# Eighteen pieces of small TensorE work in the two mixers of a hybrid decoder step, moved to neighbouring places

## The chip, the cores and the metric

One core of a Trainium2 chip runs the whole program in one launch. The metric is the device time of that launch in microseconds (us). All tensors are float32.

## The reference, cut to what matters

A trunk of two layers is run once on a prompt of 256 tokens and once on 8 samples of one token each (264 columns together). A layer is: SwiGLU half step, mixer, SwiGLU half step, each behind an adaLN norm whose shift, scale and gate come from a conditioning vector.

```
for l in range(DEPTH):
    mod = (c @ w_ada[l] + b_ada[l]).reshape(B, N_SUB, 3, D_MODEL)
    h = ada_norm(x, norm_gain[l, 0], mod[:, 0, 0], mod[:, 0, 1])
    x = x + 0.5 * mod[:, 0, 2] * swiglu(h, w_ffn_in[l, 0], w_ffn_out[l, 0])
    h = ada_norm(x, norm_gain[l, 1], mod[:, 1, 0], mod[:, 1, 1])
    y, sa, scv, sh, sc = mixer_block(h, ...)
    x = x + mod[:, 1, 2] * y
    h = ada_norm(x, norm_gain[l, 2], mod[:, 2, 0], mod[:, 2, 1])
    x = x + 0.5 * mod[:, 2, 2] * swiglu(h, w_ffn_in[l, 1], w_ffn_out[l, 1])
```

The mixer has three branches: A (HGRN2: gated linear recurrence, 4 heads of 128), B (causal convolution and RG-LRU) and C (GLA: gated linear recurrence, 4 heads of 64 keys). Each recurrence gives outputs for the prompt and a final state (`S_t = diag(f_t) S_{t-1} + k_t v_t^T`, `o_t = S_t^T q_t`), and one step from a given state for each sample. The branch outputs are gated, merged and multiplied with `w_out`.

## The kernel before, in words

**Weights and products.** Every weight tile is loaded in float32 by a DMA of SyncE (SP), 512 KB mostly, into one of 6 slots of `raw` (`load`, L430). ScalarE (ACT) rounds it to a high part `whi` (`split_hi`, L449), VectorE (DVE) subtracts to a low part `wlo` (`split_lo`, L457), and TensorE (PE) does three products for each 128x128 block (`mm3`, L492 to L494). Such a tile is a *unit*, usually 24 matmuls of 264 columns. There are 218 units in a layer, 82 of them in the mixer. ACT and DVE prepare unit u+3 at the start of their step u, when PE has ended unit u-1; 4 slots of `whi` and `wlo`. The load of place c in SP's queue waits until the tile of place c-6 has been read by DVE (a unit) or by PE (an adaLN tile).

**The mixer's units**, in order: 0 to 3 `f`, 4 to 7 `bx`, 8 to 11 `i` (values of A), 12 to 15 `q`, 16, 17 `cq`, 18, 19 `ck`, 20 `bg`, 21 `rg wa`, 22 to 24 `bg`, 25 `rg wx`, 26 to 29 `cv` (values of C), 30 to 33 `cg`, 34 to 37 `ag`, 38 to 45 `ma`, 46 to 57 `mb` pairs with a branch unit `b` behind each (48, 51, 54, 57), 58 to 61 `mc`, 62 to 65 branch `a`, 66 to 69 `mc`, 70 to 73 branch `c`, 74 to 81 `w_out`. A unit writes one of three PSUM banks (a branch unit writes two); PE waits until the group three back in the same rotation has been read.

**Small work on PE** stands behind the matmuls of a unit, at a place that a table gives. In PE's loop over units (`mixer`) it is issued in this order: ca, alpha, transposes of the values of A and C (`values_T`, L854), levels of A then of C, a samples' output (`sample_o`, L910), then for A and after it for C: outputs (L869, L870), head sums (L918), spread (L931), transposed keys (L879), final state (`final_state`, L888); last the tail's transposes (L1042) and the adaLN group (`ada_units`, L678).

- `MIX_ADA` (L52): the four places of the adaLN groups. A group is 4 tiles, each with 4 products into 32 columns of the array (32 matmul records), and computes half of one block of 1024 outputs: the shift and the scale of the norm behind the mixer. Its four loads stand in SP's queue right behind the load of the unit three places on (`load_order`). After the second and the fourth group DVE turns the block into `mod` (`to_mod`, L1725), and after the fourth makes the gains too, at its step place+2 (`ada_ends`), last of that step.
- `AT` (L122): places of the rest, DVE's and ACT's part at the step after. `C_vT` (32, 34): the 2x4 transposes of C's values; ACT copies them at 33 and 35. `A_S` 63: the final state of A, ACT copies it at 64. `so` (24, 28, 38, 44, 47, 52): the samples' outputs of six batches of states; a batch waits for `st_new`, DVE's add of the decayed state and the outer products, which is made at its steps 24, 27, 36, 41, 46, 51.
- `PE_LV` (L239): the nine levels of each recurrence's score matrix. Level i+1 on PE waits for DVE's `keep` and `update` of level i, done at the step after level i's place. The last C level (54) is needed by C's outputs at 56.

**The samples' outer products.** DVE turns A's sample values at step 16; POOL (GpSimd) writes them to DRAM (`rows_out`, L1145), and when they have landed reads them back broadcast over the partitions (`outer`, L1159); ACT scales them by the keys at step 21 for batch 0 and at step 26 for batch 1; DVE adds them to the state at step 24 and 27; PE's output of batch 0 stands behind unit 24, of batch 1 behind unit 28. ACT and DVE take their work in order, so a wait of ACT at step 21 holds its later splits.

**The end of the mixer.** For each branch `c` unit DVE gates two tiles straight from PSUM and adds them to `tmp` (L2103, L1646, four operations). ACT makes the high part, POOL (tiles 0 to 5) or DVE (6, 7) the low part. Unit 74 takes two banks at once, those of the tiles 5 and 6 of branch `c`. In DVE's step u the split of unit u+3 stands first, the gating of unit u behind it, `ada_ends` last.

```
for u, (kind, what, j) in enumerate(MIX):
    n_unit = unit(L, "mix", u)
    if (what, j) != ("o", 0):
        split_lo(dve, n_unit + LOOK)
    ...
    ada_ends(L, "mix", u - 2)
```

Of the kernel before, what the change touches and what calls it, by code (L numbers as in the profile page):

```python
# [48 lines left out]
    return l * UNITS + BASE[stage] + k  # L49


MIX_ADA = (10, 16, 29, 71)  # L52
ADA_BLOCKS = [(0, 1), (0, 0)]
ADA_FIRST = {}
RING = 8
# [3 lines left out]
def plan_ada():  # L59

    for l in range(NL):
        for f, places, blocks in (
                (0, (("in0", 16), ("in0", 28), ("in0", 41), ("out0", 11)), [(l, 2), (l, 3), (l, 4), (l, 5)]),
                (1, (("in1", 18), ("in1", 36), ("out1", 11)), [(l, 8), (l + 1, 0), (l + 1, 1)])):
            if f:
                for n, place in enumerate(MIX_ADA):
                    ADA_FIRST[(l, "mix", place)] = (8 * len(ADA_BLOCKS) + 4 * n, 4)
# [51 lines left out]
LOAD_AT = {load: c for c, load in enumerate(LOADS)}  # L119


AT = {'ca': 9, 'alpha': 11, 'A_vT': 14, 'A_sT': 16, 'C_sT': 30, 'C_vT': (32, 34), 'A_out': 50, 'C_out': 56, 'A_kT': 59, 'A_S': 63, 'C_kT': 68, 'C_S': 70, 'tailT': 73, 'kv': (23, 26, 35, 40, 45, 50), 'st_f': ((13, 14), (15, 16), (31, 32), (36, 37), (43, 44), (48, 48)), 'k_v': ((21, 21), (26, 26), (34, 35), (39, 40), (44, 45), (49, 50)), 'so': (24, 28, 38, 44, 47, 52), 'st': (14, 17, 33, 37, 44, 48)}  # L122
EARLY_AT = {'A_abs': 7, 'A_ln': 9, 'A_ls': 9, 'A_exp': 10, 'A_k': 11, 'A_f': 10, 'C_z': 10, 'C_ln': 15, 'C_ls': 16, 'C_f': 19, 'conv': (9, 10, 14, 15), 'conv_hi': 18, 'conv_lo': 19, 'A_qs': 15, 'C_qs': 17}
HEAD_AT = {'A': {'sq': 51, 'ms': 52, 'root': 54, 'inverse': 54, 'spread': (55, 56), 'scaled': (56, 58), 'high': 59, 'low': 59}, 'C': {'sq': 57, 'ms': 59, 'root': 62, 'inverse': 62, 'spread': (64, 67), 'scaled': (64, 67), 'high': 67, 'low': 67}}

# [36 lines left out]
def mixer_groups():  # L162

    out = []
    for u, (kind, what, j) in enumerate(MIX):
# [5 lines left out]
        elif kind == "br":  # L171
            out += [(e, "br" + what, 2 * j + n, u) for n in range(2)]
        out += [("V", "so", i, u) for i in (4, 5) if AT["so"][i] == u]
    return out
# [61 lines left out]
LEVELS = [0, 1, 2, 4, 8, 16, 32, 64, 128]  # L236


PE_LV = {'A': (17, 20, 24, 28, 31, 33, 38, 43, 45), 'C': (24, 28, 33, 38, 43, 45, 47, 50, 54)}  # L239
RG_AT = {'tanh': 22, 'gate': 25, 'exp': 26, 'square': 28, 'scaled': 30, 'root': 29, 'u': 32, 'scan': 32, 'y': 35, 'high': 37, 'low': 37}  # L240


# [3 lines left out]
def trunk(nc, x_prompt, x_sample, c_prompt, c_sample, state_hgrn, state_conv, state_rglru, state_gla,  # L246
# [4 lines left out]
    with ctx:  # L251
# [150 lines left out]
        def wait(eng, name, L, i=0):  # L402

            eng.wait_ge(S[name], L * PER[name] + i + 1)
# [62 lines left out]
        def group_done(eng, L, stage, g):  # L467

            g += G_BASE[(L, stage)]
            e = EV[g]  # L470
            eng.wait_ge(evac[e], ev_count(e, g + 1))
# [164 lines left out]
        def _(pe):  # L636
# [148 lines left out]
            def ca_sums(L):  # L785

                pe.wait_ge(alpha_in, (L + 1) * 80)
                for j in range(4):
                    for kt in (2 * j, 2 * j + 1):
                        last = mm(AUX[3][32 * j:32 * j + 32, 0:NT], wca[:, kt, :], tmp[:, kt], start=(kt % 2 == 0),  # L790
                                  stop=(kt % 2 == 1))
                last.then_inc(S["ca_mm"], 1)

            def alpha(L):

                wait(pe, "ca_done", L)
                pe.wait_ge(set_pool, 4)
                for jj in range(2):
                    last = mm(AUX[2][:, jj * 256:jj * 256 + 256], wal[:, jj * P:(jj + 1) * P],
                              ca[:, 0:256], start=True, stop=True)  # L800
                for jj in range(2):
                    last = mm(AUX[3][:, jj * 8:jj * 8 + 8], wal[:, jj * P:(jj + 1) * P],
                              ca[:, 256:264], start=True, stop=True)
                last.then_inc(S["C_alpha"], 1)
# [87 lines left out]
            def sample_o(L, i, bank):  # L892
                br, j = BATCHES[i]
                wait(pe, "st_new", L, i)
                if i == 0:
                    wait(pe, "A_sc", L, 0)
                    wait(pe, "A_qs", L)
                else:
                    wait(pe, "soe", L, i - 1)
                if i == 2:  # L900
                    wait(pe, "C_vTe", L, 1)
                if i == 5:
                    wait(pe, "A_oe", L)
                if i == 4:
                    wait(pe, "C_qs", L)
                for e in range(1 if br == "A" else 2):
                    rows_ = slice(0, P) if br == "A" else slice(64 * e, 64 * e + 64)
                    q_ = qs[rows_, j if br == "A" else 4 + j]
                    for n in range(4):
                        last = mm((AUX[1], bank)[e][32 * n:32 * n + 32, 0:256].rearrange("p (b v) -> p b v", b=NB), q_,  # L910
                                  st[rows_, i % 2, :, 32 * n:32 * n + 32], start=True, stop=True)
                last.then_inc(S["so"], 1)
# [22 lines left out]
            def mixer(L):  # L935
                g = [0]

                def take_bank():
                    if g[0] < 3:
                        group_done(pe, L, "out0", 4 + g[0])  # L940
                    if g[0] >= 3:
                        group_done(pe, L, "mix", g[0] - 3)
                    g[0] += 1
                    return BK[(g[0] - 1) % 3]


                for u, (kind, what, j) in enumerate(MIX):
# [46 lines left out]
                    if u == 2:  # L994
# [6 lines left out]
                        group_done(pe, L, "out0", KT - 1)  # L1001
                    if u == AT["ca"]:
                        ca_sums(L)
                    if u == AT["alpha"]:
                        alpha(L)
                    if u == AT["A_vT"]:
                        wait(pe, "rows_evac", L)
# [3 lines left out]
                    for t in range(2):  # L1011
                        if u == AT["C_vT"][t]:
                            if t == 0:
# [5 lines left out]
                    for br in "AC":  # L1019
                        for li in range(9):  # L1020
                            if u == PE_LV[br][li]:
                                level(L, br, li)
                    for i in range(6):
                        if u == AT["so"][i]:
                            sample_o(L, i, take_bank() if i >= 4 else None)
# [618 lines left out]
        def _(dve):  # L1644
# [265 lines left out]
            def mixer(L):  # L1910
# [107 lines left out]
                for u, (kind, what, j) in enumerate(MIX):  # L2018
# [150 lines left out]
                    for br in "AC":  # L2169
                        for li in range(9):  # L2170
                            if u == PE_LV[br][li] + 1:
                                keep(br, li)
# [145 lines left out]
```

## Time and profile before

| what | value |
|---|---|
| median of 3 runs (lowest, highest) | 1465.27 us (1463.87, 1466.27) |
| the profiled execution, its time and span | 1464.36 us, span 1462.6 us |
| PE busy, weight loads, DVE, ACT, POOL | 98%, 94%, 63%, 55%, 6% of the span |
| mean granted clock of PE | 0.994 |
| share of PE in the chain that ended last | 89% |
| DMA | 323.77 MB, mean 221 GB/s |
| mixer of layer 0, of layer 1 (first unit to last) | about 253 to 536 us, 964 to 1250 us |

PE's busy share says little alone: matmuls overlap, each record is about 0.28 us long and a new one starts every 0.12 us. What an interruption costs is read from the distance between starts. A row of the timeline merges equal instructions that follow one another; in brackets stands the idle time of the engine before it and what ended it.

### The profile page before, as it was taken

Reading aid. Unit: us, or ns where it says so; the run is one execution under the profiler, and the core shown is the slowest. Engines: PE = TensorE matmul, PEld = TensorE weight load, DVE = VectorE, ACT = ScalarE, POOL = GpSimd, SP = SyncE. Lnnn points to the kernel's source line nnn. Section 1 sums busy time; section 2 is a strip of 40 time slices with the busy share of each in tenths; the row PEclk is TensorE's granted clock in tenths of the full one; section 3 lists DMA queues with packets and bytes.
Section 4 is the critical chain, followed back from the end, with each engine's and each line's share of the span. In section 5 each row is a group of like instructions: output and inputs, shape, how many; then the busy total and the mean of one; then the engine's idle time right before and its main releaser. Section 6 shows DMA issues by size and latency. Waiting matters only on the chain.

```text
span 1462.6 us, 33414 instructions
## 1 busy us (share of the span) xinstructions
PE 1433.3 (98%) x14126; PEld 1372.0 (94%) x14126; DVE 923.8 (63%) x1572; ACT 807.5 (55%) x1337; POOL 86.9 (6%) x131
## 2 busy tenths in 40 slices
PE   6999999999999999999999999999899999999998
PEld 4999999998999999999999999999899999999998
DVE  3564546778876677555575554577797677855553
ACT  2554435886666466444464444468766655644543
POOL 1030000001110110000000000000011002000000
PEclk9999999999999999999999999999999999999999
DMA  9988897688884669788668888777889557775661
GB/s 341 292 260 265 249 265 196 174 251 256 228 228 142 191 176 293 217 248 252 185 202 264 271 269 266 189 187 209 234 238 268 164 152 208 219 241 157 180 187 41
DMA packets 460039, 323.77 MB, mean 221 GB/s; under 512 B 11220, under 2 KB 435708, under 8 KB 459891
## 3 DMA queue, kind: packets, MB, share of 16 engines
q1 hardware_dynamic: 452240, 299.96, 70.0%
q0 software_dynamic: 6880, 20.41, 4.9%
q8 instruction: 112, 1.84, 0.5%
q10 hardware_dynamic: 770, 1.27, 0.2%
q14 instruction: 37, 0.30, 0.1%
HBM read 313.29 MB, written 8.37 MB: 220 GB/s over the span
## 4 chain that ended last, share of the span: by engine, by line
PE 89%; ACT 3%; DMA 3%; DVE 2%; issue 2%; SPq 1%; POOL 0%; DVEq 0%; ACTq 0%; POOLq 0%
PE bank L492 27%; PE bank L493 26%; PE bank L494 26%; PE bank L678 4%; DMA xA<-v_rows 1%; SPq L550 1%; ACT xA L1222 1%; ACT whi L449 1%; DMA v_rows<-vrA 1%; DMA raw<-in_w_ffn_in 1%; DVE st L1646 1%; PE bank L869 1%; PE bank L888 1%; DVE wlo L457 0%; PE bank L910 0%
## 5 line engine op out<-in xcount | busy, mean ns | idle before, releaser
L457 DVE TENSOR_TENSOR wlo<-raw,whi 128x1024 fp32r<-128x1024 f32 (+1 forms) x436 | 518.6, 1203 | 357.9 <-ACT whi L449 356.8
L492 PE MATMUL bank<-hH,whi 128*128 128x264 f32 x2048 | 588.6, 287 | 1.1 <-DVE hL L1646 0.6
L493 PE MATMUL bank<-hL,whi 128*128 128x264 f32 x2048 | 582.0, 284 | 0.0
L494 PE MATMUL bank<-hH,wlo 128*128 128x264 f32 x2048 | 581.3, 284 | 0.0
L449 ACT ACTIVATE whi<-raw 128x1024 fp32r<-128x1024 f32 (+1 forms) x436 | 442.1, 1033 | 187.7 <-PE bank L494 178.3
L492 PEld LDWEIGHTS bank<-hH,whi 128*128 128x128 f32 x2048 | 387.1, 189 | 14.9 <-issue 13.6
L493 PEld LDWEIGHTS bank<-hL,whi 128*128 128x128 f32 x2048 | 387.5, 189 | 0.0
L494 PEld LDWEIGHTS bank<-hH,wlo 128*128 128x128 f32 x2048 | 385.6, 188 | 0.0
L492 PE MATMUL bank<-hidH,whi 128*128 128x264 f32 x704 | 201.1, 286 | 0.0
L494 PE MATMUL bank<-hidH,wlo 128*128 128x264 f32 x704 | 200.1, 284 | 0.0
L493 PE MATMUL bank<-hidL,whi 128*128 128x264 f32 x704 | 199.5, 283 | 0.0
L492 PEld LDWEIGHTS bank<-hidH,whi 128*128 128x128 f32 x704 | 132.4, 188 | 1.6 <-issue 1.2
L1222 ACT ACTIVATE hidH<-hid 128x264 fp32r<-128x264 f32 x88 | 37.3, 424 | 173.1 <-DVE hid L1646 173.0
L494 PEld LDWEIGHTS bank<-hidH,wlo 128*128 128x128 f32 x704 | 132.7, 188 | 0.0
L493 PEld LDWEIGHTS bank<-hidL,whi 128*128 128x128 f32 x704 | 132.3, 188 | 0.1
L492 PE MATMUL bank<-uH,whi 128*128 128x274 f32 x320 | 94.4, 295 | 0.0
L493 PE MATMUL bank<-uL,whi 128*128 128x274 f32 x320 | 92.8, 290 | 0.0
L494 PE MATMUL bank<-uH,wlo 128*128 128x274 f32 x320 | 92.4, 289 | 0.0
L1222 ACT ACTIVATE sil<-bank 128x264 f32<-128x264 f32 x76 | 29.8, 392 | 96.4 <-PE bank L494 96.4
L492 PE MATMUL bank<-yH,whi 128*128 128x264 f32 x256 | 73.8, 288 | 1.3 <-DVE gA L2103 1.3
L494 PE MATMUL bank<-yH,wlo 128*128 128x264 f32 x256 | 72.7, 284 | 0.0
L493 PE MATMUL bank<-yL,whi 128*128 128x264 f32 x256 | 72.6, 284 | 0.0
(323 smaller groups left out, 1656.8 us busy)
## 6 DMA issues: line engine op xcount, KB each, us to landing
raw<-in_w_ffn_in SPq DMA_DIRECT2D x176, 512.0 KB, 4.8
raw<-in_w_in SPq DMA_DIRECT2D x120, 512.0 KB, 4.8
ring<-in_w_ada SPq DMA_DIRECT2D x96, 512.0 KB, 6.6
raw<-in_w_ffn_out SPq DMA_DIRECT2D x64, 512.0 KB, 4.8
raw<-in_w_ada SPq DMA_DIRECT2D x32, 512.0 KB, 4.3
raw<-in_w_ffn_out SPq DMA_DIRECT2D x32, 384.0 KB, 4.7
first<-in_w_ada SPq DMA_DIRECT2D x16, 512.0 KB, 12.3
raw<-in_w_out SPq DMA_DIRECT2D x16, 512.0 KB, 4.9
```

The costliest lines, as they stand in the source:

```text
L449: nc.scalar.activation(whi[:, s, 0:w], raw[:, r, 0:w], ACT.Copy).then_inc(hi_done, 1)
L457: nc.vector.tensor_tensor(wlo[:, s, 0:w], raw[:, r, 0:w], whi[:, s, 0:w].bitcast(F), ALU.subtract).then_inc(lo_done, 1)
L492: nc.tensor.matmul(out, a, rh, start=start, stop=False)
L493: nc.tensor.matmul(out, a, rl, start=False, stop=False)
L494: return nc.tensor.matmul(out, b, rh, start=False, stop=stop)
L550: sp.dma_start(first[:, n], src).then_inc(first_in[FIRST_OF[n]], 16)
L678: last = mm(ps[32 * j:32 * j + 32, 0:256].rearrange("p (b i) -> p b i", i=32), cst[:, kt], src[:, j], start=(kt == 0), stop=(kt == KT - 1))
L869: mm(o, v0, sc[br][:, h, 0:T], start=True, stop=False)
L888: last = mm(AUX[base][0:dk, h * P:(h + 1) * P], KTT[br][:, t, h * dk:(h + 1) * dk], VT[br][:, t, h * P:(h + 1) * P], start=(t == 0), stop= ...
L1222: return nc.scalar.activation(out, in_, func, **k)
L1646: tt = lambda o, i0, i1, op: v.tensor_tensor(o, i0, i1, op)
```

## The change

Nine entries of three tables get a new value, for both mixers. Nothing is added or taken away; the arithmetic is the same.

```diff
-MIX_ADA = (10, 16, 29, 71)
+MIX_ADA = (11, 17, 28, 70)
...
-AT = {... 'C_vT': (32, 34), ... 'A_S': 63, ... 'so': (24, 28, 38, 44, 47, 52), ...}
+AT = {... 'C_vT': (31, 33), ... 'A_S': 64, ... 'so': (24, 28, 38, 43, 47, 52), ...}
...
-PE_LV = {'A': (17, 20, 24, 28, 31, 33, 38, 43, 45), 'C': (24, 28, 33, 38, 43, 45, 47, 50, 54)}
+PE_LV = {'A': (17, 20, 24, 28, 31, 33, 38, 43, 45), 'C': (24, 28, 33, 38, 43, 45, 47, 50, 52)}
```

Where each piece stands then: adaLN groups behind alpha (11), behind A's level 0 (17), behind two levels and the samples' output of batch 1 (28), behind C's final state (70). C's value transposes in front of A's level at 31 and of two levels at 33. A's final state in front of C's first spread (64). The samples' output of batch 3 behind two levels (43). C's last level in front of the samples' output of batch 5 and A's head sums (52). The steps of ACT and DVE that follow a place, and the adaLN loads in SP's queue, move with it.

## Rows read from the trace of the kernel before

**Rows 1.** PE's waits: who waited for whom: total us, times, longest

```profile
PE bank L910 <- DVE st L1646: 7.7, 4, 2.5
...
PE bank L492 <- DVE gA L2103: 1.3, 2, 0.7
```

**Rows 2.** PE's timeline: the samples' output of batch 0, layers 0 and 1 (start, us)

```profile
330.46 0.64 PE L910 MATMUL bank<-st,qs 128*32 128x256 f32 x8 [0.72 <-DVE st L1646]
...
1042.93 1.08 PE L910 MATMUL bank<-st,qs 128*32 128x256 f32 x8 [2.09 <-DVE st L1646]
```

**Rows 3.** A window behind the wait at unit 28: us, busy times, PEclk (granted clock), DMA

```profile
346.20:349.60 3.40, 3.40 (x16) 3.40 (x17) 3.37 (x5) 0.00 (x0) 0.00 (x0) 0.50 0.79 255
```

**Rows 4.** PE's timeline: the adaLN group behind unit 16, layer 0 (start, us)

```profile
301.93 0.28 PE L493 MATMUL bank<-hL,whi 128*128 128x264 f32 x1
302.05 0.28 PE L494 MATMUL bank<-hH,wlo 128*128 128x264 f32 x1
302.26 1.93 PE L678 MATMUL bank<-raw,cst 128*32 128x256 f32 x32
304.12 0.39 PE L492 MATMUL bank<-hH,whi 128*128 128x264 f32 x1
304.35 0.29 PE L493 MATMUL bank<-hL,whi 128*128 128x264 f32 x1
```

**Rows 5.** PE's timeline: a samples' output behind a level (38), and alone (44)

```profile
383.45 0.64 PE L910 MATMUL bank<-st,qs 128*32 128x256 f32 x8
384.02 0.39 PE L492 MATMUL bank<-hH,whi 128*128 128x264 f32 x1
...
403.57 0.64 PE L910 MATMUL bank<-st,qs 128*32 128x256 f32 x8
404.14 0.39 PE L492 MATMUL bank<-hH,whi 128*128 128x264 f32 x1
```

**Rows 6.** PE's timeline: eight transposes alone, and eight in front of head sums

```profile
295.50 1.04 PE L854 MATMUL bank<-ident,vA 128*128 128x128 f32 x8
296.29 0.37 PE L492 MATMUL bank<-hH,whi 128*128 128x264 f32 x1
...
460.96 1.04 PE L879 MATMUL bank<-ident,kA 128*128 128x128 f32 x8
461.92 0.65 PE L918 MATMUL bank<-xA,ones 128*32 128x264 f32 x8
```

**Rows 7.** ACT's timeline: step 19 and 21 of layer 0, step 21 of layer 1

```profile
313.11 1.06 ACT L449 ACTIVATE whi<-raw 128x1024 fp32r<-128x1024 f32 x1 [0.61 <-DMA raw<-in_w_in]
...
320.59 2.46 ACT L1222 ACTIVATE xA<-xA,kA 128x128 f32<-128x128 f32 x8 [0.39 <-DMA xA<-v_rows]
...
1033.06 2.46 ACT L1222 ACTIVATE xA<-xA,kA 128x128 f32<-128x128 f32 x8 [1.84 <-DMA xA<-v_rows]
```

**Rows 8.** DVE's timeline, step 17 of layer 0: the low part of unit 20

```profile
308.00 1.23 DVE L457 TENSOR_TENSOR wlo<-raw,whi 128x1024 fp32r<-128x1024 f32 x1 [0.18 <-ACT whi L449]
```

**Rows 9.** SP's loads (L430) issued from 300 to 312 us

```profile
DMA to landing us min/median/max: 3.1/6.1/8.2
```

**Rows 10.** DVE's timeline: steps 71 to 74 of layer 0

```profile
503.82 0.43 DVE L2103 SCALAR_TENSOR_TENSOR gA<-xA,bank 128x264 f32<-128x264 f32 x1 [2.06 <-PE bank L494]
...
508.82 0.43 DVE L2103 SCALAR_TENSOR_TENSOR gA<-XB,bank 128x264 f32<-128x264 f32 x1 [1.60 <-PE bank L494]
...
510.44 1.78 DVE L457 TENSOR_TENSOR wlo<-raw,whi 128x1024 fp32r<-128x1024 f32 x1
512.15 0.41 DVE L2103 SCALAR_TENSOR_TENSOR gA<-XB,bank 128x264 f32<-128x264 f32 x1
...
513.85 0.44 DVE L1725 STREAM_TRANSPOSE adaT<-bank 128x256 f32<-128x256 f32 x1
...
514.74 0.77 DVE L1646 TENSOR_TENSOR yL<-tmp,yH 128x264 fp32r<-128x264 f32 x2
```

**Rows 11.** PE's timeline: the first matmul of unit 74, layer 0

```profile
512.82 0.36 PE L492 MATMUL bank<-yH,whi 128*128 128x264 f32 x1 [0.65 <-DVE gA L2103]
```

More of the change, by code:

```diff
@@ L119 @@
 LOAD_AT = {load: c for c, load in enumerate(LOADS)}
-AT = {'ca': 9, 'alpha': 11, 'A_vT': 14, 'A_sT': 16, 'C_sT': 30, 'C_vT': (32, 34), 'A_out': 50, 'C_out': 56, 'A_kT': 59, 'A_S': 63, 'C_kT': 68, 'C_S': 70, 'tailT': 73, 'kv': (23, 26, 35, 40, 45, 50), 'st_f': ((13, 14), (15, 16), (31, 32), (36, 37), (43, 44), (48, 48)), 'k_v': ((21, 21), (26, 26), (34, 35), (39, 40), (44, 45), (49, 50)), 'so': (24, 28, 38, 44, 47, 52), 'st': (14, 17, 33, 37, 44, 48)}
+AT = {'ca': 9, 'alpha': 11, 'A_vT': 14, 'A_sT': 16, 'C_sT': 30, 'C_vT': (31, 33), 'A_out': 50, 'C_out': 56, 'A_kT': 59, 'A_S': 64, 'C_kT': 68, 'C_S': 70, 'tailT': 73, 'kv': (23, 26, 35, 40, 45, 50), 'st_f': ((13, 14), (15, 16), (31, 32), (36, 37), (43, 44), (48, 48)), 'k_v': ((21, 21), (26, 26), (34, 35), (39, 40), (44, 45), (49, 50)), 'so': (24, 28, 38, 43, 47, 52), 'st': (14, 17, 33, 37, 44, 48)}
 EARLY_AT = {'A_abs': 7, 'A_ln': 9, 'A_ls': 9, 'A_exp': 10, 'A_k': 11, 'A_f': 10, 'C_z': 10, 'C_ln': 15, 'C_ls': 16, 'C_f': 19, 'conv': (9, 10, 14, 15), 'conv_hi': 18, 'conv_lo': 19, 'A_qs': 15, 'C_qs': 17}
```

## The prediction

> **What bounds the kernel now.** I read the chain that ended last first: PE holds most of it, so time is won or lost where PE starts its next matmul later or earlier. PE's waits come next. In the mixers only two kinds are long: the samples' outputs wait four times for DVE's new state, 7.7 us in all, and the first unit of `w_out` waits twice for DVE's gating of branch c, 0.7 us each [rows 1]. Of the four, the one behind unit 24 is 0.72 us in layer 0 and 2.09 in layer 1 [rows 2]; those behind unit 28 take the rest, 2.5 each. The windows show what the first kind costs besides: after the wait at unit 28 the granted clock is 0.50, the 1.2 GHz level, for 3.4 us [rows 3]; half of it, 1.7 us, is lost. The trace has one behind each of the three waits over 2 us; in layer 1 the output of batch 0 itself runs in it (1.08 us instead of 0.64), in layer 0, after 0.72 us, it doesn't [rows 2]. Everything else in the mixer is PE going from unit to unit, and the timeline gives the price of a stop there.
>
> **What a stop costs.** Matmuls of a unit start 0.12 us apart. Before the adaLN group it is 0.21, and after the first matmul behind it 0.23 [rows 4]. So work that uses 32 columns of the array costs itself (304.12 - 302.26 = 1.86 us for the group) plus 0.09 at the entry and 0.11 at the exit. A samples' output takes 0.57 us to the next unit whether it stands alone or behind a level [rows 5], so one that joins saves the 0.20. Full-width work is different: eight transposes take 0.79 us alone plus 0.08 behind them, 0.87 together, and 0.96 when 32-column work follows, 0.09 of it the entry of the follower that is paid anyway [rows 6]. A join with them saves nothing.
>
> The Trainium skill, page TensorE: Matmul & The Clock Gate, section Part 2: What happens when you issue a matmul, speaks against the change: the next weights are pulled ahead and loaded beside a running matmul, so a switch would be hidden. The trace doesn't agree for 32-column work, 0.21 against 0.12 us. By the page all joins would bring 0.0; this is the third rival.
>
> **The change part by part**, for one mixer:
> - adaLN group to 17, to 28, to 70; samples' output to 43; C's last level to 52: each joins other small work: 5 x 0.20 = 1.0 us. The last follows no 32-column work but precedes it; the same pair of edges goes.
> - adaLN group to 11: behind alpha, which is full width: between 0.0 [rows 6] and 0.20 [rows 4]; I take the middle, 0.1.
> - C's transposes to 31 and 33, A's final state to 64: full width in front of narrow work: 0.0 as in rows 6, at most 0.1 each, below nothing only if a wait appears. The four transposes (half of 0.87 us) now delay the level behind them; DVE takes that level a step later, behind a split and a gating, which cover it.
>
> Sum of the joins: 1.1 us. But not all of it reaches the end.
>
> **Absorbed at the samples' outputs.** The 0.3 us of the groups at 11 and 17 lie before the wait at 24. That wait is not set by PE: ACT's products of batch 0 wait for the broadcast that POOL fetched, 0.39 us in layer 0 and 1.84 in layer 1 [rows 7], and DVE's and PE's parts follow ACT's queue from there. PE arrives 0.3 earlier and waits 0.3 longer: nothing is won. The wait at 28 hangs on ACT's queue after unit 26, so it moves with PE and stays 2.5 us [rows 1].
>
> **SP's queue.** Each group takes its four 512 KB loads one place along. At 17 this matters: the load of unit 22 stood behind an adaLN tile six places back and could go at once; now it waits for the low part of unit 20, done at 308.00 + 1.23 = 309.2 us [rows 8]. Loads here land 3.1 to 8.2 us after issue [rows 9], so at 312.3 to 317.4; before, ACT took it at 313.11 [rows 7]. I take 4.5 us (only one 256 KB load stands before it, while the median of 6.1 is of loads queued in a burst): 313.7, so ACT is 0.6 later. In layer 0 ACT has 0.4 of slack before the broadcast, so the samples' output comes 0.2 later; in layer 1 it has 1.8. Against that, POOL's small writes and its broadcast meet two 512 KB loads less in their first 2 us, and may land up to 1 us earlier; only layer 1 can use that. I take +0.2 and -0.2: 0 in all, with 1 us either way for each mixer. At 11 the load of unit 16 goes later in the same way, but DVE's wait for alpha goes 2 us earlier, and ACT has idle time until step 15. At 28 unit 32's load is taken late by ACT and DVE, three units before PE needs it. The groups' own tiles are released a step later, like the group. POOL can fetch the last state batch one unit earlier, since it waits for the output of batch 3; nobody waits for it.
>
> **New at unit 74.** This is the costly part. The group at 71 stood between units 71 and 72, now it stands before unit 71. So unit 71 ends 1.86 us later, while unit 72 ends at the same time as before less 0.20. DVE's gating of unit 71 begins at 503.82 + 1.86 = 505.68 us [rows 10]. Four operations take 510.44 - 508.82 = 1.62, the split behind them 512.15 - 510.44 = 1.71: 509.01, now later than unit 72's end allows (508.82 less 0.20 = 508.62). Four more operations: 510.63. Then comes what stood behind unit 73's gating and moves to step 72: the turn of the adaLN block and the gains, 514.74 - 513.85 = 0.89: 511.52. The next split, 1.71: 513.23, and there the tile's gating starts that stood at 512.15. PE's unit 74 follows 512.82 - 512.15 = 0.67 behind it [rows 10, 11]: 513.90, against 512.82. That is 1.08 us later, and it has already swallowed the 0.20 of the group at 70. The split takes 1.78 us here and 1.23 elsewhere [rows 10, 8]; it is slow while POOL makes low parts beside it. If the second one escaped POOL it would be 0.5 instead of 1.1; if the turn is slowed as well, 1.4. Unit 72 and 73 themselves don't wait: their banks are those of tiles gated two units earlier.
>
> The Trainium skill, page SBUF — State Buffer, section Who interferes with whom, says that a DVE instruction with two SBUF inputs contends with a GpSimd one that reads SBUF. By that rule, the trace agrees (1.78 against 1.23).
>
> **Other queues.** DVE's step 44 has batch 3's output in front of a level's work, whose taker is a unit away; its step 53 gets C's last level from step 55, behind the reading of batch 5, and what follows there is idle time. C's last level at 52 waits for DVE's level 7 of step 51, one unit after the step's start instead of three. No wait of that kind stands in the list of before for a level at such a distance; the nearest bounds are 0 and the 0.7 of the other DVE wait [rows 1]. I take 0, since DVE has a whole unit of PE for four short operations. The turn of the block at step 18 moves to 19, behind the low parts that unit 21 waits for: that helps if anything.
>
> **Sum.** Joins that count: samples' output 0.20, level 0.20, group at 28 0.20: 0.6 us for a mixer. Unit 74: +1.1. Net +0.5, for two mixers +1.0 us. The profiled execution took 1464.36 us (span 1462.6 and 1.8 around it), so this execution would take 1465.3; it stands 0.9 under the median of 1465.27, and the median becomes 1466.2. The measurement can tell about 0.2% (2.9 us) from no change, so I forecast no change.
>
> **Rivals.**
> 1. Joins as priced, and DVE hides the later step 71 (it has 2.06 and 1.60 us of idle time there [rows 10]). For it: idle time exists. Against: it lies before the operands come. Then 2 x (-0.8) = -1.6: 1463.7. Chance 0.17.
> 2. Slower: the late load. If unit 22's load takes the 6.1 us of the median, it lands at 315.3, 2.2 us after 313.11. Layer 0's samples' output is then 1.8 later, layer 1's 0.4 (slack 1.8). Unit 21 waits too, since the low parts of the convolution stand behind unit 22's split in DVE's queue. With +1.0 that is +3.2: 1468.5; at 7 us of landing +5.0. It decides from 5.9 us of landing on. For it: DMA runs near its full rate behind this point. Against: the burst is shorter. Chance 0.13.
> 3. Joins save nothing: +2 x 1.1 = 2.2: 1467.5. Against: rows 4 and 5. Chance 0.05.
> 4. Faster: one slow-clock stretch goes. In layer 1 the wait at 24 is 2.1 us and brings one [rows 2, 3]; in layer 0 it is 0.7 and brings none. If the broadcast lands 1 us earlier the wait is near 1.1: -1.0 - 1.7 + 1.0 = -1.7, and with rival 1's end -4.3: 1461.0. Chance 0.10, half of it over the bound. The stretch could come in layer 0 instead: 1.7 the other way, in the range.
> 5. The change doesn't do what it says: a moved piece waits where it stands now (0.05); no more than 1 us by the slack above.
>
> My own forecast has 0.50. **Chances:** faster 0.10, same 0.78, slower 0.12. **Range:** 1462.5 (joins of full-width work 0.1 each, 0.5 at unit 74, one stretch less) to 1469.5 (rival 2 with 6.5 us).
>
> **What would show it.** PE's timeline: L678 behind L802, L841, L910 and L888 with no unit between; the 0.21 before it gone at 17, 28, 70. PE's wait for DVE's gating is 1.7 to 1.9 us instead of 0.7, and the turn of the block (L1725) in front of the split before tile 6's gating. The waits for the new state about 8.3 us in four, the one at 28 unchanged at 2.5. ACT's idle time before unit 22's split 1.0 to 1.5 us instead of 0.6. The prediction is wrong if unit 74's wait stays at 0.7, if a wait appears at a level, or if the granted clock is low in two or four stretches instead of three.

## The result, and the profile after it

| what | before | after |
|---|---|---|
| median of 20 runs each (lowest, highest) | 1463.93 us (1459.72, 1466.43) | 1467.56 us (1466.35, 1472.62) |
| ratio after / before, 95% interval | | 1.0031 [1.0023, 1.0039] |
| the profiled execution: time, span | 1464.36, 1462.6 | 1466.35, 1464.6 |
| mean granted clock of PE in it | 0.994 | 0.995 |

The kernel is slower, by 3.6 us between the medians and 4.5 us by the ratio (3.4 to 5.7 by its interval). The forecast was +1.0 us on a median of 1465.27, too little to be told from no change (2.9 us). The measured time lies inside the range, but on the side to which I gave 0.12.

First PE's waits of the kernel after (the columns are those of [rows 1]):

```profile
PE bank L910 <- DVE st L1646: 5.3, 4, 2.5
...
PE bank L492 <- DVE gA L2103: 4.9, 4, 2.0
...
PE bank L845 <- DVE xC L1646: 1.7, 2, 0.8
PE bank L910 <- issue: 0.7, 1, 0.7
PE bank L678 <- DMA raw<-in_w_ada: 0.6, 2, 0.4
...
PE bank L492 <- ACT tmp L1222: 0.6, 2, 0.4
```

Against [rows 1] the wait for the new state has fallen from 7.7 to 5.3 us, and the wait for DVE's gating has grown from 1.3 us in two to 4.9 in four. New in the list are the waits of C's level (L845, 0.18 us each before) and of an adaLN group for its own tile (L678).

Then the end of each unit on PE, taken from the timelines of the two profiled executions. The table gives how much the step of each unit has grown (+) or shrunk (-), the steps of the units named added up:

| piece, by the units around its place | predicted | layer 0 | layer 1 |
|---|---|---|---|
| adaLN group to 11 (units 11, 12) | -0.1, absorbed | -0.11 | -0.11 |
| adaLN group to 17 (17, 18) | -0.2, absorbed | +0.24 | +0.15 |
| samples' output of batch 0 (25), low clock included | 0 | +0.76 | -3.12 |
| adaLN group to 28 (29, 30) | -0.20 | -0.18 | -0.21 |
| C's transposes to 31, 33 | 0.0 | -0.01 | -0.02 |
| samples' output to 43 (44, 45) | -0.20 | -0.20 | -0.20 |
| level behind unit 47 (48) | 0 | +0.65 | +0.61 |
| C's last level to 52 (53, 55) | -0.20 | -0.18 | -0.18 |
| A's final state to 64 (64, 65) | 0.0 | +0.76 | +0.79 |
| adaLN group to 70, unit 74 | +1.1 | +1.13 | +1.14 |

With +0.27 at unit 21 of layer 1 the columns add up to the +2.0 us between the two profiled executions. So the trace shows two losses of 0.6 to 0.8 us in each mixer and one of 0.8 at batch 0 of layer 0 that the prediction does not have, and one gain of 3.1 us in layer 1 that it had only as a rival. The medians differ by more than these two executions do (3.6 us); that rest is in no trace of this pair.

**Unit 74**, PE's, DVE's and POOL's timelines of the kernel after, layer 0:

```profile
502.32 1.93 PE L678 MATMUL bank<-raw,cst 128*32 128x256 f32 x32
504.18 0.39 PE L492 MATMUL bank<-zH,whi 128*128 128x264 f32 x1
...
515.68 0.36 PE L492 MATMUL bank<-yH,whi 128*128 128x264 f32 x1 [1.97 <-DVE gA L2103]
```

```profile
507.42 0.43 DVE L2103 SCALAR_TENSOR_TENSOR gA<-xA,bank 128x264 f32<-128x264 f32 x1 [3.13 <-PE bank L494]
...
509.05 1.78 DVE L457 TENSOR_TENSOR wlo<-raw,whi 128x1024 fp32r<-128x1024 f32 x1
510.76 0.41 DVE L2103 SCALAR_TENSOR_TENSOR gA<-XB,bank 128x264 f32<-128x264 f32 x1
...
512.46 0.44 DVE L1725 STREAM_TRANSPOSE adaT<-bank 128x256 f32<-128x256 f32 x1
...
513.29 0.67 DVE L1749 SCALAR_TENSOR_TENSOR Gs<-mod,par_all 128x72 f32<-128x72 f32 x1
513.88 1.21 DVE L457 TENSOR_TENSOR wlo<-raw,whi 128x1024 fp32r<-128x1024 f32 x1
515.01 0.42 DVE L2103 SCALAR_TENSOR_TENSOR gA<-XB,bank 128x264 f32<-128x264 f32 x1
```

```profile
512.27 1.59 POOL L1203 TENSOR_TENSOR yL<-tmp,yH 128x264 fp32r<-128x264 f32 x2 [0.82 <-ACT yH L1222]
```

The first product of the group starts 0.20 us behind the last one of C's final state, as unit 71's did before, so the group brings no edge of its own: units 71 and 72 together take 0.18 us less (+1.87 - 2.05). DVE's gating of unit 71 begins at 507.42 behind an idle time of 3.13 us (2.06 in [rows 10]); from there DVE has no idle time until the gating that unit 74 waits for. The span from the one to the other is 7.59 us; the prediction's steps give 513.23 - 505.68 = 7.55. Two of its terms are off and cancel. The turn and the gains take 513.88 - 512.46 = 1.42 us instead of 0.89, with the same three operations: POOL's low parts (512.27 to 513.86) now run beside them, the gains (L1749) above all. In the kernel before, POOL had ended at 512.83, ahead of the turn at 513.85. DVE's and POOL's timelines of the kernel before:

```profile
514.59 0.23 DVE L1749 SCALAR_TENSOR_TENSOR Gs<-mod,par_all 128x72 f32<-128x72 f32 x1
```

```profile
510.33 2.50 POOL L1203 TENSOR_TENSOR yL<-tmp,yH 128x264 fp32r<-128x264 f32 x2 [2.49 <-ACT yH L1222]
```

The split behind the turn then starts just when POOL ends, and takes 1.13 us to the next start instead of 1.71.

**The level behind unit 47.** The timeline of ACT, DVE and PE together, of the kernel before and then of the kernel after:

```profile
403.67 0.39 ACT L1222 ACTIVATE XB<-bank 128x264 f32<-128x264 f32 x1 [2.33 <-PE bank L494]
...
409.88 1.23 DVE L457 TENSOR_TENSOR wlo<-raw,whi 128x1024 fp32r<-128x1024 f32 x1 [0.62 <-ACT whi L449]
...
414.81 0.18 DVE L1646 TENSOR_TENSOR xC<-xC 128x16 f32<-128x16 f32 x1
...
415.04 0.46 PE L845 MATMUL bank<-qC,kC 64*32 64x32 f32 x32 [0.18 <-DVE xC L1646]
```

```profile
404.93 0.39 ACT L1222 ACTIVATE XB<-bank 128x264 f32<-128x264 f32 x1 [2.91 <-PE bank L494]
...
411.02 1.23 DVE L457 TENSOR_TENSOR wlo<-raw,whi 128x1024 fp32r<-128x1024 f32 x1 [1.17 <-ACT whi L449]
...
415.96 0.17 DVE L1646 TENSOR_TENSOR xC<-xC 128x16 f32<-128x16 f32 x1
...
416.19 0.46 PE L845 MATMUL bank<-qC,kC 64*32 64x32 f32 x32 [0.84 <-DVE xC L1646]
```

PE, ACT and DVE form one line here. Unit 44 ends 0.57 us later, because the samples' output stands in front of it; ACT takes its bank later by the same (its idle time goes from 2.33 to 2.91), DVE waits longer for ACT (0.62 to 1.17), and the chain of the level ends late. PE has the 0.20 of the join in hand and arrives early: 0.18 + 0.57 + 0.20 = 0.95 was to be expected, 0.84 is the row.

**Unit 64**, DVE's and PE's timelines of the kernel after:

```profile
474.12 1.80 DVE L2223 RECIPROCAL xA<-xA 128x264 f32<-128x264 f32 x1
475.83 1.16 DVE L457 TENSOR_TENSOR wlo<-raw,whi 128x1024 fp32r<-128x1024 f32 x1
476.91 0.42 DVE L2103 SCALAR_TENSOR_TENSOR gA<-XB,bank 128x264 f32<-128x264 f32 x1
```

```profile
476.60 0.29 PE L494 MATMUL bank<-yH,wlo 128*128 128x264 f32 x1
477.38 0.39 PE L492 MATMUL bank<-yH,whi 128*128 128x264 f32 x1 [0.50 <-DVE gA L2103]
```

The second bank of unit 64 waits for the first gating of unit 63, which stands behind a reciprocal and a split. In the kernel before the final state's 1.70 us of products lay in front of unit 64 and hid that. The idle time of 0.50 us costs more than itself: 477.38 - 476.60 = 0.78 us lie between two starts, 0.66 more than the usual 0.12, and the first product behind the wait takes 0.23 us to the next start, 0.11 more. Together that is the 0.8 of the table.

**Batch 0 and POOL's queue.** POOL's timeline in layers 0 and 1, of the kernel before and of the kernel after; then PE's of the kernel after:

```profile
314.91 0.58 POOL L1159 DMA_DIRECT2D xA<-v_rows  x1 [5.15 <-DMA v_rows<-vrA]
...
1026.51 0.57 POOL L1159 DMA_DIRECT2D xA<-v_rows  x1 [5.70 <-DMA v_rows<-vrA]
```

```profile
312.76 0.58 POOL L1159 DMA_DIRECT2D xA<-v_rows  x1 [3.10 <-DMA v_rows<-vrA]
...
1027.01 0.57 POOL L1159 DMA_DIRECT2D xA<-v_rows  x1 [3.21 <-DMA v_rows<-vrA]
```

```profile
330.09 0.62 PE L910 MATMUL bank<-st,qs 128*32 128x256 f32 x2 [0.20 <-DVE st L1646]
331.37 0.63 PE L910 MATMUL bank<-st,qs 128*32 128x256 f32 x6 [0.66 <-issue]
...
1044.13 0.64 PE L910 MATMUL bank<-st,qs 128*32 128x256 f32 x8 [0.20 <-DVE st L1646]
```

POOL waits 2.1 and 2.5 us less for its four small writes. PE's wait for batch 0 is now 0.20 in both layers (0.72 and 2.09 in [rows 2]). In layer 0 nothing is won: two of the eight products start, then the engine stands 0.66 us for nothing that the profile shows. Between the two starts lie 331.37 - 330.09 = 1.28 us; less the 0.52 that the wait is shorter, that is the 0.76 of the table. In layer 1 the wait of 2 us is gone, and with it the stretch of low clock behind it, as the windows show (columns: stretch, length, busy times of PE, PEld, DVE, ACT, POOL, then PEclk, DMA share, GB/s):

```profile
346.60:350.00 3.40, 3.40 (x36) 1.70 (x32) 2.74 (x3) 0.79 (x1) 0.00 (x0) 0.50 0.84 237
1042.50:1045.90 3.40, 3.20 (x146) 2.59 (x145) 3.37 (x6) 1.81 (x4) 1.18 (x2) 1.00 0.91 272
...
515.50:518.90 3.40, 3.22 (x27) 3.25 (x27) 3.08 (x6) 2.56 (x6) 0.00 (x0) 1.00 0.64 188
```

The clock is at its upper level behind batch 0 and, in this execution, behind unit 74 too. That is one stretch less than before, worth 1.7 us; this execution is the fastest of the 20.

**The late tile.** PE's timeline, the adaLN group behind unit 17:

```profile
305.58 1.48 PE L678 MATMUL bank<-raw,cst 128*32 128x256 f32 x22
307.42 0.64 PE L678 MATMUL bank<-raw,cst 128*32 128x256 f32 x8 [0.37 <-DMA raw<-in_w_ada]
```

The group's fourth tile lands after the third is used up; that costs the 0.20 of the join and 0.2 more.

### The profile page after: what moved, and what is told of

Read it like the earlier page. It is cut to its first block, busy times and chain, and to the rows that moved or that the text cites. A ratio compares the mean times of both kernels' runs of the same rounds, so it can differ in the third digit from the quotient of the medians.

```text
span 1464.6 us, 33414 instructions
## 1 busy us (share of the span) xinstructions
PE 1431.3 (98%) x14126; PEld 1369.3 (93%) x14126; DVE 923.9 (63%) x1572; ACT 806.2 (55%) x1337; POOL 85.2 (6%) x131
## 4 chain that ended last, share of the span: by engine, by line
PE 88%; DVE 4%; ACT 3%; DMA 2%; issue 2%; SPq 1%; DVEq 0%; ACTq 0%
PE bank L492 27%; PE bank L493 26%; PE bank L494 26%; PE bank L678 4%; SPq L550 1%; DVE wlo L457 1%; ACT xA L1222 1%; DMA raw<-in_w_ada 1%; DMA raw<-in_w_ffn_in 1%; ACT whi L449 1%; DMA raw<-in_w_in 1%; PE bank L910 1%; PE bank L841 1%; PE bank L869 1%; DVE st L1646 1%
```

## The experiments

My theory after these traces: the change wins 0.2 us per join, as priced, and loses it threefold where a unit that an ACT or DVE chain waits for ends later (units 44 and 71) or loses its cover (unit 64). The main rival: the wait at unit 74 alone, with the low clock that it may bring, carries the loss. Eleven kernels were timed, each beside the kernel before, whose median was 1465.43 us beside the first four, 1464.66 beside the next four and 1464.65 beside the last three. The stated gains are the ratio times 1464.9.

### One entry alone, on the kernel before

**The last adaLN group.**

```diff
-MIX_ADA = (10, 16, 29, 71)
+MIX_ADA = (10, 16, 29, 70)
```

> The kernel before with one entry changed: the fourth adaLN group at 70 instead of 71. Theory (the piece put in front of a unit delays that unit's end for DVE and ACT): PE's wait at unit 74 goes from 0.65 to about 2.0 us in both mixers, the join saves 0.2 each, so the time is 2.3 us above the kernel before (+0.15%). Rival (the whole loss comes from loads and from stretches of slow clock): the wait at 74 stays at 0.65 and the time is 0.4 us below the kernel before.

Measured: 1467.73 us, ratio 1.0028 [1.0017, 1.0039], so +4.1 us. The wait at unit 74 is 1.98 us in layer 0 and 2.00 in layer 1, 0.65 before. Unit 74 ends 1.16 us later in layer 0 (+1.87 - 2.05 + 1.34). In layer 1 its own step is +2.88 instead of +1.34, since there the clock is low behind the wait, as PE's timeline and a window show:

```profile
1228.76 0.36 PE L492 MATMUL bank<-yH,whi 128*128 128x264 f32 x1 [2.00 <-DVE gA L2103]
```

```profile
1229.00:1232.40 3.40, 3.40 (x17) 3.40 (x17) 2.63 (x5) 2.58 (x6) 0.00 (x0) 0.51 0.58 167
```

This one entry is the largest loss. The later unit 74 accounts for 2 x 1.16 = 2.3 us of it, as expected; the rest is taken up under the low clock below.

**A's final state.**

```diff
-'A_S': 63
+'A_S': 64
```

> The kernel before with one entry changed: A's final state at 64 instead of 63. Theory: unit 64 starts 1.8 us earlier against DVE, which is still held by the reciprocal of step 62, so PE waits about 0.5 us for DVE's gating in unit 64 in both mixers; the join saves nothing; +1.5 us in all (+0.1%). Rival (the wait seen there in the changed kernel is a consequence of the other moves): no wait in unit 64, time the same as before within 0.2 us.

Measured: 1465.66 us, ratio 1.0007 [0.9997, 1.0016], +1.0 us. PE's timeline has the wait in the middle of unit 64 by itself, and the units' ends give +0.8 us for a mixer:

```profile
475.71 0.39 PE L492 MATMUL bank<-yH,whi 128*128 128x264 f32 x1 [0.50 <-DVE gA L2103]
```

So this entry alone brings the wait; no kernel with A's final state at 63 has it. The time by itself does not tell +1.0 from nothing.

**The samples' output of batch 3.**

```diff
-'so': (24, 28, 38, 44, 47, 52)
+'so': (24, 28, 38, 43, 47, 52)
```

> The kernel before with one entry changed: the samples' output of batch 3 at 43 instead of 44. Theory: unit 44 ends 0.57 us later, ACT's chain of step 44 starts from its end, the split of unit 49 and with it DVE's step 46 come 0.6 to 0.7 us later, and PE's wait for C's decay at place 47 goes from 0.2 to 0.8 us in both mixers; the join gives back 0.2; +0.9 us in all. Rival (DVE's reading of the batch in step 44 is the cause): the same wait, but ACT's split of unit 49 is not late against PE's unit 45. Rival (SP's queue): no wait, -0.4 us.

Measured: 1465.73 us, ratio 1.0008 [0.9999, 1.0016], +1.2 us. The wait at the level behind unit 47 is 0.85 us in layer 0 and 1.37 in layer 1; the step of unit 44 is +0.57, the two of 44 and 45 together -0.20, that of unit 48 +0.65 in layer 0 and +1.14 in layer 1. The wait varies from one execution to the next, so I took it from all 13 profiles of this case: with the output at 44 it is 0.15 to 1.43 us, mean 0.40 (18 places), with the output at 43 it is 0.83 to 1.37, mean 0.91 (8 places). The entry costs 0.5 us of waiting for a mixer and wins 0.2. The time by itself does not tell +1.2 from nothing. Against the kernel before, ACT's split of unit 49 starts 1.25 us later in layer 0 (410.05 instead of 408.80), unit 46's bank only 0.59 (412.59 instead of 412.00), and DVE waits 1.17 us for a split of ACT instead of 0.62. So ACT is late against PE, and the rival that DVE's reading of the batch is the cause falls.

**The first two adaLN groups.**

```diff
-MIX_ADA = (10, 16, 29, 71)
+MIX_ADA = (11, 17, 29, 71)
```

> The kernel before with the first two adaLN groups at 11 and 17 instead of 10 and 16. Theory: the joins (0.1 and 0.2 us) are absorbed or lost to a late adaLN tile (0.3 us at 17); POOL's small writes land 2 to 2.5 us earlier since fewer loads run beside them; the wait for batch 0's state shrinks in layer 1 from 2.1 to below 0.5 us and with it one stretch of slow clock goes: between 0 and -3 us against the kernel before. Rival (the late load of unit 22 costs): ACT is late at step 19, the wait at unit 24 grows in both mixers, +1 to +3 us.

Measured: 1463.94 us, ratio 0.9995 [0.9984, 1.0007], -0.7 us. The tile at 17 is late (0.32 and 0.17 us), layer 0's output of batch 0 has a hole of 0.93 us, and layer 1's wait is 0.21 instead of 2.09 with its low clock gone. The effect on batch 0 in layer 1 is thus due to these two entries. Unit 21 takes 0.13 and 0.29 us more with them.

**The third group and C's last level.**

```diff
-MIX_ADA = (10, 16, 29, 71)
+MIX_ADA = (10, 16, 28, 71)
-'C': (24, 28, 33, 38, 43, 45, 47, 50, 54)
+'C': (24, 28, 33, 38, 43, 45, 47, 50, 52)
```

> The kernel before with only the third adaLN group at 28 and C's last level at 52. Theory (a join of 32-column work saves 0.2 us and these two make no wait): 4 x 0.2 = 0.8 us below the kernel before. Rival (the Trainium skill's pull-ahead hides the switch): no difference. Rival (a wait at C's last level): an idle stretch before it at 52, and slower.

Measured: 1462.69 us, ratio 0.9989 [0.9977, 1.0000], -1.6 us, with no new wait. Two joins of 0.18 in two mixers make 0.7; the rest is inside the interval.

The five sum to +4.1 + 1.0 + 1.2 - 0.7 - 1.6 = +4.0 us, against +4.5 for the whole change. Each has an interval of 1.2 to 1.7 us either way, so the agreement is a weak check. C's transposes, not tried alone, are 0.0 in the table.

### The costly entries taken back, and the turn of the block

**The change without its three costly entries**, on the kernel after:

```diff
-MIX_ADA = (11, 17, 28, 70)
+MIX_ADA = (11, 17, 28, 71)
-'A_S': 64, 'so': (24, 28, 38, 43, 47, 52)
+'A_S': 63, 'so': (24, 28, 38, 44, 47, 52)
```

> The changed kernel with the three suspected entries undone (fourth group 71, A's final state 63, batch 3's output 44). Theory: 2 x (1.1 + 0.75 + 0.45) = 4.6 us below the changed kernel, 0 to 1 us below the kernel before, waits at 47, 64 and 74 as before. Rival (the moved loads at 11, 17 and 28 carry the loss): still 2 us or more above the kernel before.

Measured: 1461.67 us, ratio 0.9978 [0.9966, 0.9990]: 3.2 us under before and faster than both kernels. Unit 74 waits 0.65 again. That is 5.9 us under the kernel after by the medians and 7.8 by the ratios, more than the 4.6 expected, and more under before than the 0 to 1 expected; the traces leave this rest open.

**The same with the last group at 70:**

```diff
-MIX_ADA = (11, 17, 28, 71)
+MIX_ADA = (11, 17, 28, 70)
```

> The faster mixture (last adaLN group at 71, A's final state at 63, batch 3 at 44) with the one entry for the last adaLN group set to 70. Theory: the group at 70 is worth +1.1 us a mixer by PE's starts at unit 74 (idle 1.9 to 2.0 us instead of 0.65), so +2.3 us, and up to 1.7 us more for each mixer where a wait of 2 us brings a low-clock stretch: 1464 to 1467 against the mixture's 1461.7, and the gap that is left to the kernel after (1467.6) is that of batch 3 and of A's state, 2 to 3 us. Rival (the entries add up otherwise, the group at 70 carries the whole loss): 1467 or more, the same as the kernel after.

Measured: 1463.98 us, ratio 0.9999 [0.9988, 1.0011], 2.3 us above the mixture without it by the medians. The waits at unit 74 are 2.07 and 1.98. That is the theory's size for the waits; the rival, that this entry alone brings the time of the kernel after, falls. In layer 0 of this execution the low clock stands behind unit 74 and not behind unit 28 (in layer 1 it is the other way round):

```profile
515.50:518.90 3.40, 3.40 (x18) 3.40 (x17) 1.49 (x2) 1.65 (x4) 0.00 (x0) 0.50 0.45 133
346.00:349.40 3.40, 3.12 (x46) 2.02 (x47) 3.24 (x4) 0.35 (x1) 0.00 (x0) 1.00 0.75 196
```

**The turn of the block one step later**, on the kernel after:

```diff
-                    ada_ends(L, "mix", u - 2)
+                    ada_ends(L, "mix", u - (3 if u > 70 else 2))
```

> The changed kernel, but DVE turns the adaLN block of the fourth group at its step 73 again, as before, with the group itself at 70. Theory (the turn in front of the split of unit 76 is about 1.4 of the 1.3 to 1.5 us added to the wait, the late end of unit 71 only fills DVE's idle time): the wait at 74 falls from 1.98 to 0.6 to 0.9 us, 2 to 2.7 us below the changed kernel. Rival (the late end of unit 71 is the cause): the wait stays at 1.5 us or more and the time falls by under 1 us.

Measured: 1463.93 us, ratio 0.9991 [0.9982, 1.0000]; 3.6 us under the kernel after by the medians, 5.9 by the ratios. The wait at unit 74 is 1.13 us in both layers, so 0.85 of the 1.98 was the turn and 0.48 the late end of unit 71. Both parts count: I had expected 0.6 to 0.9 us of waiting if the turn were all, and 1.5 or more if the late end were. DVE's timeline tells why the turn is worth only 0.85 when it takes 513.88 - 512.46 = 1.42:

```profile
512.15 1.78 DVE L457 TENSOR_TENSOR wlo<-raw,whi 128x1024 fp32r<-128x1024 f32 x1
```

Without the turn in front, the split falls beside POOL's low parts again and takes 1.78 us; with it, it starts at 513.88, just when POOL ends (512.27 + 1.59 = 513.86), and takes 1.21.

### The low clock

**Dummy products in the wait at unit 74**, on the kernel after, four products of ones into a bank that nobody reads:

```diff
                     unit_ready(pe, n)
+                    if u == 74:
+                        keep_warm(4)
```

> The kernel after, with four more 128x256 products of ones (eight matmul records, about 1.8 us of work, into a bank that nobody reads) ahead of unit 74's wait for DVE. Theory (the wait of 2.0 us costs its own length and, in some executions, a stretch at half the clock on top): unit 74 starts where it started, 0.0 to 0.1 us later; the idle time in front of it falls from 1.97 us to about 0.2; no low-clock stretch begins behind it; the time is 0 to 1.7 us under the kernel after in each mixer where such a stretch came in its runs, so 0 to 3.4 us under it. Rival (the wait costs only its length, the rest of the measured +4.5 us lies elsewhere): the same time as the kernel after, 1467.5, or up to 0.3 us more.

Measured: 1465.69 us, ratio 1.0007 [0.9997, 1.0017]; 1.9 us under the kernel after by the medians, 3.5 by the ratios. PE's timeline: the products fill the pause, and unit 74 follows.

```profile
513.36 1.89 PE L712 MATMUL bank<-ones 128*128 128x256 f32 x8
515.34 0.36 PE L492 MATMUL bank<-yH,whi 128*128 128x264 f32 x1
```

**Dummy products in the wait at unit 28**, on the faster mixture:

```diff
+                    if u == 28:
+                        keep_warm(5, BK[3], T)
                     for i in range(6):
                         if u == AT["so"][i]:
                             sample_o(L, i, take_bank() if i >= 4 else None)
```

> The faster mixture (the kernel after with its last adaLN group kept at 71, A's final state at 63, batch 3's output at 44) with five more 128x256 products of ones (ten records, about 2.2 us) ahead of the samples' output of batch 1 behind unit 28, where PE waits 2.4 us for DVE's new state. Theory (the stretch of low clock follows from PE's pause): the wait falls to about 0.2 us, the output starts where it started, both stretches of 3.4 us at 0.5 are gone and the time is 2 x 1.7 = 3.4 us under that mixture's 1461.7, so about 1458. Rival 1 (the low clock comes from elsewhere, such as the load on the whole array): stretches stay, time the same, 1461.7. Rival 2 (the pause was covered work for nothing: PE's products delay the output or the levels behind it): the output starts later than in the mixture by the overrun, the time is 1462 or more.

Measured: 1460.27 us, ratio 0.9977 [0.9968, 0.9986]. By the medians it is 1.4 us under the mixture, by the ratios 0.1; the theory had 3.4. The trace shows the mechanism whole: the adaLN group behind the output takes 1.91 us where the mixture has 3.52, the clock is 1.00, and unit 29 ends 1.63 and 1.67 us earlier. PE's timelines, of this kernel, then of the mixture:

```profile
344.32 2.42 PE L712 MATMUL bank<-ones 128*128 128x256 f32 x10
346.86 0.64 PE L910 MATMUL bank<-st,qs 128*32 128x256 f32 x8
347.31 1.91 PE L678 MATMUL bank<-raw,cst 128*32 128x256 f32 x32
```

```profile
347.62 0.64 PE L910 MATMUL bank<-st,qs 128*32 128x256 f32 x8 [2.46 <-DVE st L1646]
348.07 3.52 PE L678 MATMUL bank<-raw,cst 128*32 128x256 f32 x32
```

**Clock and work apart.** Each run lists its time and its mean granted clock. The time multiplied with the clock is roughly what the run would take at full clock; the rest is what the low clock took at most (part of it lies at the kernel's ends). Means over the runs of a kernel:

| kernel (runs) | time | clock | at full clock | lost |
|---|---|---|---|---|
| before (93) | 1464.8 | 0.9939 | 1455.9 | 9.0 |
| after (20) | 1468.3 | 0.9936 | 1458.9 | 9.4 |
| after, unit 74's wait filled (11) | 1465.9 | 0.9952 | 1458.9 | 7.1 |
| after, turn later (12) | 1463.8 | 0.9952 | 1456.8 | 7.1 |
| last group at 70 alone (8) | 1468.2 | 0.9929 | 1457.8 | 10.5 |
| mixture (12) | 1462.2 | 0.9946 | 1454.3 | 7.9 |
| mixture, last group at 70 (11) | 1464.6 | 0.9945 | 1456.6 | 8.0 |
| mixture, unit 28's wait filled (11) | 1460.6 | 0.9965 | 1455.4 | 5.2 |

The standard error of a value at full clock is 0.14 us for before and 0.3 to 0.6 for the others. Filling unit 74's wait changes nothing at full clock and gives back 2.3 us of low clock, with a standard error of 0.9: the theory holds there by the clocks of the runs, though the one trace of the kernel after has no low stretch behind unit 74 that could go. Filling unit 28's gives back 2.7 us of clock (0.4) and loses 1.1 at full clock. That is under two of its standard errors (0.6), and the profiled pair shows no such loss (3.6 us between their spans), so whether it is real is open. And the change as a whole costs 3.1 us at full clock and 0.4 in clock: what it wins behind batch 0 of layer 1 it loses again elsewhere, at unit 74 above all, as the kernel with that wait filled shows. The last group alone costs 1.9 and 1.5 us; added to the mixture it costs 2.3 and 0.1. The work at full clock is 2 x 1.13, the clock is what varies.

**The wait at unit 28 filled with the adaLN group itself**, on the kernel before:

```diff
-MIX_ADA = (10, 16, 29, 71)
+MIX_ADA = (10, 16, 27, 71)
```

> The kernel before with only the third adaLN group moved, to 27, in front of the wait for batch 1's state behind unit 28, instead of 29. Theory (that wait hangs on ACT's queue after unit 26 and not on PE): the group's 1.86 us fall into it, it drops from 2.5 to about 0.6 us in both mixers, and the two stretches of slow clock behind it go (1.7 us each): 2 x (1.9 + 1.7) = 7 us below the kernel before. Rival (the wait moves with PE, since ACT's part follows PE's units): the wait stays at 2.5 us and the time is the same. Rival between: the wait falls but the slow clock stays: -4 us.

Measured: 1464.41 us, ratio 0.9997 [0.9986, 1.0008]. The wait for the state falls from 2.46 to 0.39 and 0.35 us, and another takes its place at the level behind unit 33, 0.83 us in layer 0 and this in layer 1 (PE's timeline):

```profile
1077.91 0.74 PE L841 MATMUL bank<-qA,kA 128*32 128x16 f32 x64 [3.06 <-DVE xA L1646]
```

The 7 us that I expected did not come. It is the same lesson: unit 28, behind the group, ends later by the group, ACT's and DVE's steps with it, and what was saved comes back in the next level. By the time nothing is won.

## Why the prediction was right or wrong

- **The number** is in the range by luck. The range reached up to 1469.5 for a late load (rival 2), and what filled it were costs that the prediction put at nothing. That the median of 1467.56 is the 1467.5 of rival 3 is chance too, since the joins do save. "I forecast no change", with 2.9 us as the bound, failed: the ratio gives 3.4 to 5.7 us.
- **The joins** were right in kind and size: 0.18 to 0.21 us at 28, 43 and 52 for the 0.20 taken, 0.11 at 11 for the middle value 0.1, 0.0 for the transposes. The rival that joins save nothing falls, since the steps of the units there are shorter by these amounts. The 0.21 in front of 32-column work is not gone everywhere, as I had written it would be: the group at 70 still starts 0.20 us behind the product before it, but the next unit stood there at 0.20 before. The Trainium skill, page TensorE: Matmul & The Clock Gate, section Part 2: What happens when you issue a matmul, which would have the switch hidden, isn't borne out by these rows.
- **Unit 74** was right: 1.13 us for the 1.08 forecast, with a wait of 1.97 and 1.98 us for the 1.7 to 1.9. The path was right, and the closeness was partly luck. Two terms inside were off and cancelled: the turn and the gains ran beside POOL and took 1.42 us, not 0.89, and the split behind them escaped POOL and took 1.13 us to the next start instead of 1.71. The prediction had named both ("if the turn is slowed as well", "if the second one escaped POOL"), but each alone. The Trainium skill, page SBUF — State Buffer, section Who interferes with whom, was cited for the contention; by that rule, the trace agrees again, on both sides: 1.78 us beside POOL, 1.21 the moment POOL ends. Rival 1, that DVE hides the later step, falls: its idle time lies before the operands come, as said against it.
- **The low clock at unit 74 is missing in that step.** I priced one stretch leaving (rival 4), and none coming there, though the wait I forecast, 1.7 to 1.9 us, was near the 2.09 of [rows 2] that brought one. It comes in some executions: in the traces behind 2 of the 6 waits of about 2 us there. By the clocks of the runs it is worth between 0.1 and 2.3 us over both mixers.
- **"A's final state to 64: 0.0"** failed. I looked at what the move joins and not at what it uncovers: 1.7 us of products had covered the gating behind a reciprocal. Measured +0.8 for a mixer; the sentence "below nothing only if a wait appears" named the condition, and its row was not looked up.
- **"DVE's step 44 has batch 3's output in front of a level's work, whose taker is a unit away"** failed as well. The delay doesn't come by DVE's reading at all; it comes by unit 44, which ends 0.57 later, and by ACT's step behind it. In this pair of traces that is +0.65 and +0.61 against the 0.20 won, in the mean of all traces +0.5. For the group at 70 I had taken exactly this path into account; for the output at 43 I didn't.
- **SP's queue.** Unit 22's load took 4.1 us where 4.5 was taken, and ACT's idle time before its split was 0.68 and 0.86 us, less than the 1.0 to 1.5 forecast. Rival 2 falls as a whole; where it looked for a wait, at unit 21, 0.08 and 0.27 us came. POOL's transfers gained 2.1 and 2.5 us where I allowed 1, so rival 4's mechanism came true in layer 1, and the wait fell to 0.20. "Absorbed at the samples' outputs" fails in layer 1, and in layer 0 the shorter wait (0.52 us) was more than eaten by the break in the middle of the output (1.28 us between the two starts), whose cause is open. That the group itself could wait for its own fourth tile at 17 was not in the prediction: I followed the loads behind the group and not the group's own.
- **The sum.** Predicted +0.5 for a mixer. Without batch 0 the traces give +2.1 and +2.2. The terms that I lacked are A's state with 0.8, the level behind unit 47 with 0.6, and the late tile with 0.2. In layer 1 the 0.3 at unit 21 comes on top. Batch 0 gives +0.8 in layer 0 and -3.1 in layer 1.

## What to carry to other kernels

A piece of 32-column work that moves one unit forward and joins other small work makes the stream 0.2 us shorter here, but the unit it now precedes ends later by the piece's whole length, and every step of the other engines that starts at that unit's end is late by that length: price each move as both. Ask of each piece, too, what it covered where it stood. And take each entry of a table of places on its own: here three of nine, timed one by one, lost 6.3 us (4.1, 1.0 and 1.2; the last two are shown by their waits and not by the time), and the other six together won 3.2.

## What was not expected of the hardware

- Over the 13 profiled executions, stretches at 0.50 inside the mixers begin behind 23 of 35 pauses of PE of 1.58 to 3.06 us, and behind none of six pauses of 1.13 to 1.43 us. The same pause, 2.46 us at unit 28, has one in 15 of 22 cases: a pause makes the low clock likely, not certain. Every such stretch stood behind a pause.
- When PE waits only 0.2 us for batch 0 in layer 0, its output breaks off after two products for 0.33 to 0.93 us without a releaser ("issue"). It does so in layer 0 of all seven kernels with the first two groups moved, and not in layer 1; with the third group at 27, where the wait for batch 1 was short, the hole of 0.69 us stood in that output, again in layer 0 alone. The cause was not tried.
- POOL waits 2.1 and 2.5 us less for its four small writes when the first two groups' loads stand one place later in SP's queue. The kernel with these two entries alone shows the same (3.13 and 3.33 us), so they are the cause; which of the two, and that it is by their loads, was not tried.
